# RWKV-7 triangular inversion on one core: the second products of each level with 32 moving columns in place of 64

## What is computed

```python
def _rwkv7_scan(r, decay, k, v, kk, b):
    """State S[i(value), j(key)]:
    S_t = S_{t-1} diag(decay_t) - (S_{t-1} kk_t) b_t^T + v_t k_t^T ;  y_t = S_t r_t."""
    def step(S, inp):
        r_t, w_t, k_t, v_t, kk_t, b_t = inp
        sa = jnp.einsum('bhij,bhj->bhi', S, kk_t)
        S = S * w_t[:, :, None, :] - sa[..., None] * b_t[:, :, None, :] + v_t[..., None] * k_t[:, :, None, :]
        y = jnp.einsum('bhij,bhj->bhi', S, r_t)
        return S, y
```

## Time and profile before

| | |
|---|---|
| runs | 4112.28, 4112.4, 4128.48 us |
| the profiled execution | 4112.34 us |
| its span, first to last instruction | 4110.5 us |
| mean granted TensorE clock | 0.949 of full speed |
| busy, of the span | TensorE 91%, VectorE 53%, ScalarE 21%, GpSimd 14% |
| RWKV's matmuls (L742) in the chain that ended last | 7% |
| L1555 and L1556 in that chain | 1% each |

### The profile page before, as it was taken

How to read it: one execution, slowest core, us unless ns; L and a number is a source line. 1 busy time by engine, 2 the same in 40 slices (tenths; PEclk the granted TensorE clock), 3 DMA queues, 4 the chain that set the end, 5 groups by cost and what they waited for, 6 DMA issues and landing times.

```text
span 4110.5 us, 69068 instructions
## 1 busy us (share of the span) xinstructions
PE 3755.0 (91%) x29136; PEld 2851.0 (69%) x29136; DVE 2166.3 (53%) x4280; ACT 870.3 (21%) x1768; POOL 555.6 (14%) x444
## 2 busy tenths in 40 slices
PE   7999887999979999999889998869999799999995
PEld 4566555886548888888655665558865488888884
DVE  2599745666154242434646997466661642434345
ACT  1345462332010000000113446523320100000000
POOL 0041100000011222222100411000000122222220
PEclk9999997999889999999999999879998899999997
DMA  2001100000111111112210110100001111111121
GB/s 111 26 27 41 45 22 1 3 3 26 62 62 42 42 41 42 41 51 84 79 40 21 36 36 23 33 2 3 3 26 67 57 42 41 48 45 41 42 83 52
DMA packets 43384, 163.68 MB, mean 40 GB/s; under 512 B 5056, under 2 KB 5072, under 8 KB 42720
## 3 DMA queue, kind: packets, MB, share of 16 engines
q1 hardware_dynamic: 27648, 100.68, 7.2%
q0 software_dynamic: 15456, 58.85, 3.9%
HBM read 135.07 MB, written 23.49 MB: 39 GB/s over the span
## 4 chain that ended last, share of the span: by engine, by line
PE 73%; DVE 19%; issue 4%; ACT 2%; POOL 1%; DMA 0%; DVEq 0%; ACTq 0%; POOLq 0%
PE ps L712 38%; PE ps L661 9%; PE ps L742 7%; PE ps L629 6%; DVE arena L1425 4%; PE ps L903 2%; PE ps L891 2%; PE ps L916 2%; DVE little L1455 1%; PE ps L945 1%; DVE arena L1556 1%; PE ps L673 1%; PE ps L639 1%; DVE arena L1322 1%; DVE arena L1555 1%
## 5 line engine op out<-in xcount | busy, mean ns | idle before, releaser
L712 PE MATMUL ps<-arena 128*128 128x261 f32 x4096 | 924.7, 383 | 5.7 <-POOL arena L548 2.9
L712 PEld LDWEIGHTS ps<-arena 128*128 128x128 f32 x4096 | 775.1, 189 | 135.1 <-issue 5.4
L661 PE MATMUL ps<-arena,ring 128*128 128x348 f32 x2304 | 704.5, 465 | 37.1 <-DVE arena L1301 18.9
L712 PE MATMUL ps<-arena,ring 128*128 128x261 f32 x3072 | 706.4, 385 | 21.1 <-DVE arena L1778 20.7
L712 PEld LDWEIGHTS ps<-arena,ring 128*128 128x128 f32 x3072 | 585.2, 191 | 122.1 <-issue 21.2
L661 PEld LDWEIGHTS ps<-arena,ring 128*128 128x128 f32 x2304 | 439.0, 193 | 301.4 <-issue 59.6
L742 PE MATMUL ps<-arena 64*64 64x64 f32 (+1 forms) x13600 | 513.0, 226 | 97.8 <-DVE arena L1510 43.2
L742 PEld LDWEIGHTS ps<-arena 64*64 64x64 f32 x13600 | 467.6, 135 | 142.0 <-DVE arena L1556 48.8
L1280 ACT ACTIVATE aux<-ps 128x522 f32<-128x522 f32 x64 | 38.8, 607 | 1535.0 <-PE ps L712 1535.0
L1367 DVE TENSOR_TENSOR arena<-aux,ps 128x522 f32<-128x522 f32 x160 | 111.8, 699 | 423.2 <-PE ps L712 422.7
L548 POOL TENSOR_TENSOR arena<-ring 128x512 f32<-128x512 f32 x128 | 170.1, 1329 | 1106.8 <-DMA ring<-units 1101.4
(11 more groups left out here) (228 smaller groups left out, 3674.5 us busy)
## 6 DMA issues: line engine op xcount, KB each, us to landing
ring<-units SPq DMA_DIRECT2D x192, 512.0 KB, 3.7
h_scratch<-arena POOLq DMA_DIRECT2D x24, 522.0 KB, 3.1
arena<-h_scratch POOLq DMA_DIRECT2D x24, 522.0 KB, 8.3
arena<-h_in POOLq DMA_DIRECT2D x16, 522.0 KB, 9.9
out<-arena POOLq DMA_DIRECT2D x8, 522.0 KB, 3.1
arena<-att_scratch POOLq DMA_DIRECT2D x2, 2080.0 KB, 9.3
att_scratch<-arena POOLq DMA_DIRECT2D x16, 256.0 KB, 3.1
aux<-rope POOLq DMA_DIRECT2D x2, 1044.0 KB, 12.5
```

Of the source, the lines that this page charges most:

```text
L661: ins = mm(ps[:, b + s, 0:SW], ring[:, r * D + k * P:r * D + (k + 1) * P], tile(U0, k)[:, slice_(s)], start=(k == 0), stop=(k == KT - 1))
L712: ins = mm(acc_at(n)[:, s], lhs[:, k * P:(k + 1) * P], rhs(k)[:, s * HALF:(s + 1) * HALF], start=(k == 0), stop=(k == KT // 2 - 1))
```

## The change

A view that takes every other block of 2^n columns, and its use in the second products and the subtractions. For `m` the even blocks (side 0) are moved, written and subtracted, for `mt` the odd ones (side 1). The stationary operands are the same 64x64 as before. `off` by `m`, the masks, the copies to `x`, the waits and the order of all of them stay. The lines behind the new function lie four further down in the changed file, and six further down behind the new lines of `dve_chunk`.

```diff
+        def every_other(ap, n, side):
+
+            return ap.rearrange("p (k s b) -> p k s b", s=2, b=2 ** n)[:, :, side, :]
...
                         if n < LEVELS - 1:
                             for g in pairs(half):
-                                ins = heads(half_bank(4, 7, g), mt[:, g], x[:, g])
+                                ins = heads(every_other(half_bank(4, 7, g), n, 0), mt[:, g], every_other(x[:, g], n, 0))
                             ins.then_inc(S["mx_ready"], 1)
                         for g in pairs(half):
-                            ins = heads(half_bank(2, 5, g), x[:, g], mt[:, g])
+                            ins = heads(every_other(half_bank(2, 5, g), n, 1), x[:, g], every_other(mt[:, g], n, 1))
                         ins.then_inc(S["mx_ready"], 1)
...
-                bank2 = lambda b0, b1, half: bank4(b1 if half else b0, CH)[:, 0:2]
+                part2 = lambda b0, b1, half, n, side: every_other(ps[:, b1 if half else b0, 0:P], n, side)
...
                     for half in range(2):
-                        m, mt, off, abt = (half2(k, half) for k in ("m", "mt", "off", "abt"))
+                        off, abt = (half2(k, half) for k in ("off", "abt"))
+                        m, mt = (every_other(cb(k, 256)[:, P * half:P * (half + 1)], n, side)
+                                 for side, k in enumerate(("m", "mt")))
                         if n < LEVELS - 1:
                             dve.wait_ge(S["mx_ready"], w.next("mx_ready"))
                             v.tensor_tensor(off, abt, level[n], ALU.mult)
-                            v.tensor_tensor(m, m, bank2(4, 7, half), ALU.subtract).then_inc(S["m_ready"], 1)
+                            v.tensor_tensor(m, m, part2(4, 7, half, n, 0), ALU.subtract).then_inc(S["m_ready"], 1)
                         dve.wait_ge(S["mx_ready"], w.next("mx_ready"))
-                        v.tensor_tensor(mt, mt, bank2(2, 5, half), ALU.subtract).then_inc(S["mt_ready"], 1)
+                        v.tensor_tensor(mt, mt, part2(2, 5, half, n, 1), ALU.subtract).then_inc(S["mt_ready"], 1)
```

## The result

| | before | changed |
|---|---|---|
| median of 8 runs each, in turn | 4115.95 us | 4141.93 us |
| lowest and highest | 4112.28, 4128.48 | 4122.80, 4148.01 |
| profiled execution / its span | 4112.34 / 4110.5 | 4137.22 / 4135.4 |
| mean granted TensorE clock | 0.949 | 0.936 |

The ratio of the changed kernel to the one before is 1.0056, with a 95% interval of 1.0037 to 1.0076. It is slower by about 0.6%, where 0.5% faster was predicted, and outside the predicted range of 4077 to 4110 us. The ratios in this document compare mean times, so they are not exactly the quotients of the medians shown.

The account below looks back on a forecast made before the run. The recurrences were taken as bound by a ring of TensorE, VectorE and ScalarE; 0.56 us saved in each of 34 chunks makes 19.1 us, so 4112.3 - 19.1 = 4093 us, range 4077 to 4110.

Parts of the forecast that it names:

- The pace of narrow products: Second products on TensorE: a pair of heads still takes 59 ns, set by weight loads, so no issue time saved.
- the right witness: L856, 64 moving columns with 128 weight columns at 110 ns a load, taken to show that weight loads set the pace.
- rival 1: Second products: moving columns set the pace, a pair takes 32 ns; 33 us saved, 4079 us; chance 0.09.
- The tail of 27 ns: TensorE: the last narrow product of a group ends 27 ns sooner.
- VectorE: Subtractions L1556 and L1558 shrink to 213 ns, 0.13 us from start to start; L1555 keeps its full size.
- Rival 2: VectorE's short subtractions start no sooner than 0.20 us apart; 3 us saved, 4109 us; chance 0.13.
- The turn and the chunk: Recurrences: one TensorE-VectorE-ScalarE cycle falls from 1.88 to 1.76 us, saving 0.56 us a chunk, to 17.32 us.
- The predicted way: Within a level: ScalarE's half 0 copy, 20 pairs in TensorE's queue, then the next copy limit the cycle to 1.76 us.
- the signs: Trace marks of being right: 59 ns pairs, 1.76 us cycles, 17.32 us chunks, ScalarE's copy releasing TensorE instead of L1556, clock unchanged.
- rival 3: Levels 1 to 4: short column runs slow TensorE's streams beyond the weight-load cover; up to 78 us slower, 4190 us; chance 0.12.
- The granted clock unchanged: Recurrence loops: TensorE's granted clock stays at 0.99 to 1.00, as before the change.
- Rival 4: Recurrence loops: fewer columns in flight let the clock fall to 1.2 GHz; some 370 us slower, 4490 us; chance 0.02.

Follow-up runs that it names:

- VectorE's part alone: Changed kernel with both second products moving all 64 columns again, only the subtractions narrow; median 4116.99 us against 4120.28 before, ratio 0.9984.
- one-run version: Changed kernel with the 32 columns as one run of 32 in every level (inverse not formed); median 4129.0 us, ratio 1.0034 to the kernel before.

## Why the prediction was wrong, point by point

- **The pace of narrow products: right.** 57 ns a pair was measured against 59 predicted; L856 was the right witness, and rival 1 falls. The rule of the Trainium skill ("TensorE: Matmul & The Clock Gate", "Back-to-back issue gap") that gave an estimate of 32 ns was misapplied: the section calls it the isolated gap of a single matmul and says that in a stream of weight loads and matmuls both set the spacing, so that the rule under-counts at small N. The trace agrees, with 57 ns.
- **The tail of 27 ns: right**, though the record's length does not show it. The record of a narrow product still lasts 219 to 221 ns, but it starts 0.03 us after its weight load where a wide one starts 0.06 after, so it ends sooner. And the version with wide products needs 17.38 and 17.45 us a chunk, the one with the m product narrow 17.27 and 17.34: 0.11 us for the four levels that have an m product, 27 ns each.
- **VectorE: right.** 215 and 218 ns against 213, 0.13 us from start to start (730.06 to 730.19), L1555 unchanged. Rival 2 falls.
- **The turn and the chunk: right in size, half right in the path.** 1.77 us (729.85 to 731.62) against 1.76, 17.28 and 17.35 us a chunk against 17.32; VectorE idles 0.74 us in the turn in place of 0.60. The predicted way, 20 pairs in TensorE's queue behind the copy of half 0, takes nearly as long, but the trace has a last wait of 0.02 us for the copy of half 1, and the m product's 27 ns are in the turn: with wide products it takes 1.80 us (753.14 to 754.94 in the version with VectorE's part alone). In the predicted way they would have no part. Of the signs, ScalarE's copy as releaser came out for the second products; for `off` by m the trace still names L1562 (0.17 us).
- **Short runs (rival 3): no cost.** One run of 32 and runs of 2 to 32 give the same chunk to 0.01 us. The sentence of the Trainium skill in "SBUF — State Buffer" that any non-contiguous PSUM pattern slows matmuls significantly is contradicted here for runs of at least two fp32 columns. A slower stream would be hidden under the weight load at first, but the m product's tail lies in the turn and would have shown it. How matmuls that do not wait for weights fare, no run shows.
- **"The granted clock unchanged": wrong, and this is the step that failed.** Rival 4 was the right mechanism. I gave it 0.02, because the loop "held 0.99 to 1.00 with its waits" and its records cover nine tenths of it. Those rows say what the engine was granted with 64 columns and nothing about how much less would do. The busy share could not tell: it counts a record from its start to its end, waits for weights included, and it is 0.94 in the changed kernel's loop at full clock (81.08 of 86.60 us). Columns moved in a chunk fell (144 of its 448 records move 32 fewer), and the busy share did not. What the runs showed in place of the unchanged clock: with the products of levels 1 and 2 narrow it falls to the 1.2 GHz level in level 2 of some chunks.
- **The size of rival 4: wrong too.** I priced a clock low in the whole loop, 370 us. What happened is a fall at one place of the chunk, in 8 of 34 chunks: 27 us, which gives 4093 + 27 = 4120 us. No row of the trace of before gives that number.
- **The rest of the 4137 us of the profiled execution, 17 us, was put at nothing without a reason**: the prediction takes for granted that stages outside the recurrences cost the same. The stretch between them took 13.6 us more, as low clock, the stretches ahead and behind 2 us, and the shorter turns brought 18.2 us and not 19.1. It is so with no slow chunk as with some. Why there was more low clock stays open.

## What to carry to other kernels

Work that TensorE does inside the shadow of a weight load costs no time, and taking it out gives none; but it may be what keeps the clock up. So narrow the operand where the next engine waits for the result (here VectorE, and the m product), leave the rest wide, and look at the granted clock of the loop chunk by chunk, since an average over a loop (0.94 in the one-run version) hides chunks at 1.00 and chunks near 0.75. This advice rests on one kernel. Before a gain of half a per cent is believed or denied, add up the time at the low clock in the stages whose code did not change, and compare many runs: here half of that time explains nearly their whole difference.

## What was not expected of the hardware

- The clock fell though TensorE never waited longer than 0.60 us ahead of the fall, and the kernel before waits as long without a fall. The Trainium skill ("TensorE: Matmul & The Clock Gate", "Loop structure matters more than you think") ties the fall to long waits between bursts; the trace shows one without.
- Once it had fallen it fell again at nearly the same place of three to five chunks in a row, and then no more in that recurrence. With wide products behind the place it fell singly.
- Stages whose code did not change had 201.4 us at the low clock in one version and 204.8 to 235.5 in others, in the same stretch. Added work ahead of them changed it, but not in one direction, and the runs of one version differ by as much. What decides it stays open, and so does how the first stretch can differ by 9 us between two profiles of one kernel (686.5 and 695.4).
